# Output tile transposes one step later, down tiles gated by their own 512 tokens, one gate/up load moved ahead of the down stage

## Chip, cores and metric

The kernel runs as one program on the 8 NeuronCores of one Trainium2 chip. Each core computes 2048 of the 16384 tokens. There is no communication between the cores. The metric is the device time of the slowest core in microseconds (us). TensorE is called PE, VectorE DVE, ScalarE ACT, GpSimd POOL and SyncE SP.

## What is computed

The reference is one decoder layer; the stages before the output projection are untouched by the change and cut here to a line.

```python
# ... h = rms_norm(x); q, k, v, u, gates = h @ w_in; dilated attention; pooling;
# merged = gate_a * (o_attn @ w_proj_attn) + gate_p * (y_pool @ w_proj_pool)
x = x + rms_norm(merged @ w_out[l], g_post_mix[l])

h2 = rms_norm(x, g_pre_ffn[l])
gu = h2 @ w_gate_up[l]
a, b = gu[..., :FFN_HIDDEN], gu[..., FFN_HIDDEN:]
x = x + rms_norm((jax.nn.silu(a) * b) @ w_down[l], g_post_ffn[l])
```

D_MODEL is 1024 and FFN_HIDDEN is 2816. The products run in bf16 and accumulate in float32.

## The kernel before, in words

Every engine has its own list of instructions. The order on an engine is the order in which the Python code appends to its list, and an engine does them strictly in that order; a wait on a semaphore holds back everything that stands behind it on the same engine. The DMA issues of POOL and SP stand in these lists too.

**The output projection stage.** The 2048 tokens of a core are 16 tiles of 128. `wout_step(it)` is a software pipeline over them. In one step the parts work on different tiles:

- stage 1, tile `it`: SP loads the residual `xin` (four buffers), PE does the 16 matmuls of 128x512 with `wout` (L988) into one of three pairs of PSUM banks.
- add, tile `it-3`: POOL adds `tb` and `xin` into `x1b` (L1001, three buffers), SP stores `x1b` to `x1s` in DRAM.
- 2b1, tile `it-4`: ACT squares and sums `x1b` (L359) and the reciprocal root follows. For the first tiles it is a square root on ACT (L339) with a reciprocal on DVE (L340); for the last ones it is two small instructions on POOL (L341, L343).
- 2a, tile `it-1`: ACT squares and sums the matmul result in PSUM (L359), the same reciprocal root, and DVE scales the result into `tb` (L996).
- 2b2, tile `it-5`: DVE scales `x1b` to the bf16 tile `xs` (L1040, two buffers, named `xs2` in the code), PE transposes it in 8 instructions (L1048) into one of two PSUM banks, DVE copies it with a gain into `hT` (L1050).

A buffer of `x1b` may be written again when the `xs` made from it is done and its store has landed, so the add of tile n waits for the `xs` of tile n-3.

**The gate/up stage.** It follows twice (`hf` 0 and 1), each time for 1024 tokens, over 22 chunks j of 128 hidden columns and 2 blocks b of 512 tokens. A unit (j, b) is 8 matmuls for the gate (L1144) and 8 for the up part (L1147) in one of two pairs of banks. ACT does the SiLU into `sa` (L1158), DVE multiplies into `ffT` (L1159). The pair of banks is free again when this product is done. The weights of a chunk come by a DMA from the POOL list: `issue_gu(idx+2)` stands at the head of chunk `idx`, into one of three buffers, and waits until the last matmuls on that buffer are done. The same place issues one of the 22 pieces of `wdn`. The steps 16 to 20 of `wout_step` (no stage 1 any more) are mixed into the first five units: matmuls of the unit, then the step, then SiLU and product of the unit.

**The down stage.** After the 44 units of a half, 8 tiles of 128 tokens are multiplied with `wdn` (L1176, 44 matmuls of 128x512 each), followed by a norm on ACT, POOL and DVE, and by the residual add on POOL (L1001, into the same buffers `x1b`). Every down tile waits for this:

```python
ev_ff = dve.last()
...
pe.wait(frp, bank_free[pr_[0]], bank_free[pr_[1]], ev_wd, ev_ff)
```

`ev_wd` is the landing of all pieces of `wdn`; `dve.last()` is the product of the last unit (j = 21, b = 1).

Of the kernel before, what the change touches and what calls it, by code (L numbers as in the profile page):

```python
# [14 lines left out]
NT = T // 128  # L15
HT = 2048
FF = 2816
NJ = FF // 128
# [173 lines left out]
def build_program(taps=(), stop_after=None):  # L192
# [844 lines left out]
    def wout_stage2b2(st):  # L1037
        (i, b, ev_st, col2, ev_rs) = st
        b2 = i % 2
        ev_xs = dve.op(lambda e: e.tensor_scalar(out=xs2[b2][:, :], in0=x1b[b][:, :], scalar1=rsA[:, col2:col2 + 1], scalar2=None, op0=ALU.mult),  # L1040
                       waits=[ev_rs, xs2_free[b2]])
        x1b_free[b] = [ev_xs, ev_st]
        k_, bank, fr = tr_ring2.get()
        psb = ps[:, bank, :].bitcast(BF16).rearrange("p (k t) -> p k t", k=8)
        pe.wait(ev_xs, fr, bank_free[bank])
        ev_tr = None
        for k in range(8):
            ev_tr = pe.op(lambda e, k=k: e.transpose(out=psb[:, k, :], in_=xs2[b2][:, k * 128:(k + 1) * 128], identity=ident[:, :]), signal=(k == 7))  # L1048
        xs2_free[b2] = ev_tr
        ev_ev = dve.op(lambda e: e.tensor_tensor(out=hT[:, :, i * 128:(i + 1) * 128], in0=psb, in1=gffn[:, :].unsqueeze(2).to_broadcast([128, 8, 128]), op=ALU.mult),  # L1050
                       waits=[ev_tr])
        tr_ring2.release(k_, ev_ev)
        bank_free[bank] = ev_ev
        h2_ev[i] = ev_ev
# [3 lines left out]
    boot_ev = [pool.dma(wgu_boot[i][:, :, :, :], wgu_d[i], d_gub[i]) for i in range(2)]  # L1058
    d_wd = P.dsem("d_wd")
    ev_gf = sp.dma(gfin[:, :], gfin_d[:, :], P.dsem("d_gfin"))  # L1060
    st1, st2, st3, st4 = {}, {}, {}, {}

    def wout_step(it):
        if it < NT:
            st1[it] = wout_stage1(it)
        if 0 <= it - 3 < NT:
            st3[it - 3] = wout_stage2add(st2[it - 3])
        rstd_mode["act"] = it - 4 < 12
        if 0 <= it - 4 < NT:
            st4[it - 4] = wout_stage2b1(st3[it - 4])  # L1070
        rstd_mode["act"] = it - 1 < 15
        if 0 <= it - 1 < NT:
            st2[it - 1] = wout_stage2a(st1[it - 1])
        rstd_mode["act"] = False
        if 0 <= it - 5 < NT:
            wout_stage2b2(st4[it - 5])

    for it in range(NT):
        wout_step(it)
# [13 lines left out]
    fu = 0  # L1093
# [4 lines left out]
    def issue_gu(idx):  # L1098
        hf, j = loads[idx]
        b = idx % 3  # L1100
        ld_ev[idx] = pool.dma(wgu[b][:, :, :, :], wgu_d[j], d_gu[b], waits=[gu_free[b], ev_wout])
# [23 lines left out]

    def wgu_buf(idx):
        return wgu_boot[idx] if idx < 2 else wgu[idx % 3]
    for hf in range(2):
        for j in range(NJ):
            idx = hf * NJ + j  # L1130
            if 0 < idx < len(loads) - 2:
                issue_gu(idx + 2)
            if hf == 0 and j:
                ev_wd = pool.dma(wdn[:, j, :], wdn_d[:, j, :], d_wd)
# [2 lines left out]
            for b in range(2):  # L1137
# [10 lines left out]
                               signal=(k == 7))  # L1148
                if b == 1:
                    gu_free[wb] = e2  # L1150
                if hf == 0 and fu <= 5:
                    wout_step(NT + fu - 1)
                    if fu == 1:
                        issue_gu(2)
                        pool.dma(wdn[:, 0, :], wdn_d[:, 0, :], d_wd)
                    if fu == 5:
                        obuf_free = [x1b_free[0], x1b_free[1]]
                es = act.op(lambda e, ub=ub, ba=ba: e.activation(out=sa[ub][:, :], in_=ps[:, ba, :], func=AF.Silu), waits=[e1, sa_free[ub]])  # L1158
                ef = dve.op(lambda e, ub=ub, bb=bb, j=j, b=b: e.tensor_tensor(out=ffT[:, j, b * 512:(b + 1) * 512], in0=ps[:, bb, :], in1=sa[ub][:, :], op=ALU.mult),  # L1159
                            waits=[es, e2])  # L1160
                sa_free[ub] = ef
                ab_ring.release(ka, ef)
                bank_free[ba] = ef
                bank_free[bb] = ef
        ev_ff = dve.last()
        for il in range(8):
            i = hf * 8 + il
            b = i % 2
            ev_x1 = sp.dma(xin[b][:, :], x1s_d[i * 128:(i + 1) * 128, :], d_x1i[b], waits=[xin_free[b], x1_store_ev[i]])
            kp, pr_, frp = pair_ring2.get()  # L1170
            pe.wait(frp, bank_free[pr_[0]], bank_free[pr_[1]], ev_wd, ev_ff)
            ev = None
            evh = []
            for h2 in range(2):
# [110 lines left out]
```

How the kernel before makes its waits and increments, by code:

```python
    def wait(self, *evs):  # L40
        for ev in evs:
            if ev is None:
                continue
            if isinstance(ev, (list, tuple)):
                self.wait(*ev)
                continue
            key = id(ev.sem)
            if self.seen.get(key, 0) >= ev.val:
                continue
            self.seen[key] = ev.val
            sem, val = ev.sem, ev.val
            self.meta.append(("wait", id(sem), val))
            self.ops.append(lambda e, sem=sem, val=val: e.wait_ge(sem, val))
# [1 line left out]
    def op(self, fn, waits=(), signal=True):  # L55
        self.wait(*waits)
        if signal:
            self.count += 1
            sem, val = self.sem, self.count
            self.meta.append(("inc", id(sem), 1))
            self.ops.append(lambda e, fn=fn, sem=sem: fn(e).then_inc(sem, 1))
            return Ev(sem, val)
        self.ops.append(lambda e, fn=fn: fn(e))
        return None
# [4 lines left out]
    def dma(self, out, in_, dsem, waits=(), **kw):  # L69
        self.wait(*waits)
        dsem.count += 16
        sem = dsem.sem
        self.meta.append(("inc", id(sem), 16))
        self.ops.append(lambda e, out=out, in_=in_, sem=sem, kw=kw: e.dma_start(out=out, in_=in_, **kw).then_inc(sem, 16))
        return Ev(sem, dsem.count)
```

## Time and profile before

| what | value |
|---|---|
| time, median of 3 runs | 1025.14 us (1024.16 to 1026.15) |
| time of the profiled execution | 1024.68 us |
| span of its slowest core (core 2) | 1023.1 us |
| spans of the other cores | 1013.3 to 1021.0 us (core 5 is second) |
| PE busy on core 2 | 930.6 us (91% of the span) |
| output projection stage on core 2, first L988 to the last L1048 | about 475.8 to 565.7 us |
| first down stage, second gate/up stage, second down stage | from 701.3, 777.3 and 931.3 us |

The span is counted from the first to the last instruction of a core. The time of the execution is 1.6 us more than the span. Instruction times in the trace are start and duration in us from the span's start. The end of a PE instruction is modelled, so distances on PE are read here from start to start.

### The profile page before, as it was taken

The numbers are of one execution on the slowest core, as the hardware profiler recorded it, in microseconds if no ns is written. First come the engines' busy times: TensorE is split into PE (matmuls) and PEld (weight loads), VectorE is DVE, ScalarE is ACT, GpSimd is POOL, SyncE is SP. The second block draws the span as 40 slices with busy tenths as digits, with TensorE's granted clock in tenths as the row PEclk, the third lists the DMA queues.
The fourth block names the chain that finished last, engine by engine and source line by source line (L and its number), as shares of the span: only waits on it lengthen the run. The fifth ranks groups of instructions, "written<-read, shape, count | busy, mean of one in ns | idle before, by whom it ended". The sixth has DMA issues, their size and how long they took to land.

```text
span 1023.1 us, 15111 instructions; the slowest of 8 cores (1013.3 to 1023.1 us)
## 1 busy us (share of the span) xinstructions
PE 930.6 (91%) x5448; PEld 468.4 (46%) x5532; DVE 402.5 (39%) x554; ACT 342.2 (33%) x588; POOL 334.7 (33%) x324
## 2 busy tenths in 40 slices
PE   1569999999897999999898999999999999999993
PEld 0337554447674444444444444444444444444441
DVE  2465786548978433333576212121112112121111
ACT  3426663339777422223664111111101111111100
POOL 2462787663402343333456111111333000000331
PEclk9769999999998999999999999999999999999997
DMA  8879310000022171212977766762334544530322
GB/s 233 243 173 239 80 63 21 1 1 2 4 41 43 43 124 21 42 21 42 304 240 194 118 108 117 122 108 49 124 105 139 86 71 74 83 62 1 124 104 81
DMA packets 32586, 98.50 MB, mean 96 GB/s; under 512 B 4224, under 2 KB 4224, under 8 KB 32512
## 3 DMA queue, kind: packets, MB, share of 16 engines
q0 software_dynamic: 15296, 41.92, 24.8%
q1 hardware_dynamic: 17072, 55.58, 16.3%
q8 instruction: 45, 0.74, 0.3%
q14 instruction: 29, 0.24, 0.1%
q10 hardware_dynamic: 144, 0.03, 0.0%
HBM read 122.64 MB, written 16.78 MB: 136 GB/s over the span
## 4 chain that ended last, share of the span: by engine, by line
PE 80%; DVE 5%; DMA 4%; issue 4%; POOL 3%; ACT 3%; SPq 0%; DVEq 0%; ACTq 0%; POOLq 0%
PE ps L1176 14%; PE ps L1147 14%; PE ps L1144 14%; PE ps L438 12%; PE ps L925 6%; PE ps L928 5%; PE ps L518 5%; DMA xst<-xh 2%; PE ps L988 2%; PE ps L420 2%; PE ps L935 1%; PE ps L932 1%; PE ps L482 1%; DMA xin<-xo 1%; DVE tb L996 1%
## 5 line engine op out<-in xcount | busy, mean ns | idle before, releaser
L1144 PE MATMUL ps<-hT,wgu 128*128 128x512 bf16 x658 | 157.5, 379 | 1.5 <-DMA wgu<-wgu 0.7
L1147 PE MATMUL ps<-hT,wgu 128*128 128x512 bf16 x659 | 157.6, 379 | 0.7
L1176 PE MATMUL ps<-wdn,ffT 128*128 128x512 bf16 x690 | 151.5, 379 | 2.6 <-DVE ffT L1159 1.9
L1159 DVE TENSOR_TENSOR ffT<-ps,sa 128x512 bf16<-128x512 f32 x88 | 60.8, 691 | 226.2 <-PE ps L1147 226.2
L1158 ACT ACTIVATE sa<-ps 128x512 f32<-128x512 f32 x88 | 52.5, 597 | 247.3 <-PE ps L1144 247.3
L1176 PEld LDWEIGHTS ps<-wdn,ffT 128*128 128x128 bf16 x704 | 68.8, 98 | 85.4 <-issue 2.8
L1144 PEld LDWEIGHTS ps<-hT,wgu 128*128 128x128 bf16 x672 | 65.6, 98 | 79.8 <-issue 1.2
L1147 PEld LDWEIGHTS ps<-hT,wgu 128*128 128x128 bf16 x672 | 65.8, 98 | 79.3
L74 POOL DMA_DIRECT2D wgu<-wgu x42 | 22.5, 537 | 231.9 <-PE ps L1147 228.3
L1001 POOL TENSOR_TENSOR x1b<-tb,xin 128x1024 f32<-128x1024 f32 x31 | 72.8, 2348 | 58.3 <-DVE tb L996 29.9
L438 PE MATMUL ps<-hT,wqk 128*128 128x512 bf16 x374 | 89.4, 379 | 2.0 <-DVE uh L631 1.4
L498 POOL TENSOR_TENSOR kT<-t,t2b 128x512 bf16<-128x512 f32 (+1 forms) x36 | 65.4, 1826 | 47.3 <-DVE t2b L487 43.6
L359 ACT ACTIVATE junk<-ps 128x1024 bf16<-128x1024 f32 x31 | 31.7, 1022 | 142.4 <-PE ps L1176 132.4
L996 DVE SCALAR_TENSOR_TENSOR tb<-ps,rsA,gfin 128x1024 f32<-128x1024 f32 x15 | 19.3, 1284 | 131.2 <-POOL rsA L343 131.2
L947 POOL TENSOR_TENSOR mT<-m,m 128x512 bf16<-128x512 f32 x32 | 40.5, 1266 | 86.9 <-DVE m L942 86.9
L508 ACT ACTIVATE qb<-ps 128x512 bf16<-128x512 f32 (+1 forms) x60 | 35.0, 584 | 89.8 <-PE ps L438 88.2
L925 PE MATMUL ps<-hT,wgs 128*128 128x512 bf16 x249 | 60.5, 386 | 0.5 <-issue 0.2
L928 PE MATMUL ps<-hT,wgs 128*128 128x512 bf16 x250 | 60.4, 380 | 0.3
L420 PE MATMUL ps<-ident,xsb 128*128 128x128 bf16 x256 | 23.8, 249 | 40.2 <-ACT xsb L407 22.4
L941 DVE TENSOR_TENSOR m<-ps,sga 128x512 f32<-128x512 f32 x32 | 22.1, 692 | 93.6 <-PE ps L932 88.0
L438 PEld LDWEIGHTS ps<-hT,wqk 128*128 128x128 bf16 x384 | 37.1, 98 | 44.0 <-issue 1.3
L988 PE MATMUL ps<-wout,mT 128*128 128x512 bf16 x249 | 56.7, 379 | 0.4
(120 smaller groups left out, 1195.8 us busy)
## 6 DMA issues: line engine op xcount, KB each, us to landing
wgu<-wgu POOLq DMA_DIRECT2D x42, 512.0 KB, 5.1
xst<-xh SPq DMA_DIRECT2D x16, 512.0 KB, 18.0
xin<-xo SPq DMA_DIRECT2D x16, 512.0 KB, 5.4
x1s<-x1b SPq DMA_DIRECT2D x16, 512.0 KB, 3.9
xin<-x1s SPq DMA_DIRECT2D x16, 512.0 KB, 4.1
out<-x1b SPq DMA_DIRECT2D x15, 512.0 KB, 2.9
xst<-xo SPq DMA_DIRECT2D x12, 512.0 KB, 7.1
wdn<-wdn POOLq DMA_DIRECT2D x22, 256.0 KB, 6.1
```

The source lines that it names most:

```text
L438: ev = pe.op(lambda e, k=k: e.matmul(ps[:, bank, 0:n], lhsT=wfn(k), rhs=rhsfn(k), start=(k == 0), stop=(k == 7)), signal=(k == 7))
L498: ev_o = pool.op(lambda e: e.tensor_tensor(out=dst, in0=i0, in1=i1, op=ALU.add), waits=[ev_t1, ev_t2])
L518: ev = pe.op(lambda e, k=k: e.matmul(ps[:, bank, 0:256], lhsT=tok_ap_fn(k), rhs=wv_tile[:, g, k, :], start=(k == 0), stop=(k == 7)), signa ...
L925: e1 = pe.op(lambda e, k=k, wb=wb, b1=b1, tok=tok: e.matmul(ps[:, b1, :], lhsT=wgs[wb][:, 0, k, :], rhs=hT[:, k, tok], start=(k == 0), sto ...
L928: e2 = pe.op(lambda e, k=k, wb=wb, b2=b2, tok=tok: e.matmul(ps[:, b2, :], lhsT=wgs[wb][:, 1, k, :], rhs=hT[:, k, tok], start=(k == 0), sto ...
L988: ev = pe.op(lambda e, k=k, hf=hf, pr_=pr_: e.matmul(ps[:, pr_[0] + hf, :], lhsT=mT[:, k, i * 128:(i + 1) * 128], rhs=wout[:, k, hf * 512: ...
L1001: ev_o = pool.op(lambda e: e.tensor_tensor(out=outbuf[:, :], in0=tb[b][:, :], in1=xres[:, :], op=ALU.add), waits=[ev_t, ev_xres, out_free])
L1144: e1 = pe.op(lambda e, k=k, wbuf=wbuf, ba=ba, tok=tok: e.matmul(ps[:, ba, :], lhsT=wbuf[:, 0, k, :], rhs=hT[:, k, tok], start=(k == 0), st ...
L1147: e2 = pe.op(lambda e, k=k, wbuf=wbuf, bb=bb, tok=tok: e.matmul(ps[:, bb, :], lhsT=wbuf[:, 1, k, :], rhs=hT[:, k, tok], start=(k == 0), st ...
L1158: es = act.op(lambda e, ub=ub, ba=ba: e.activation(out=sa[ub][:, :], in_=ps[:, ba, :], func=AF.Silu), waits=[e1, sa_free[ub]])
L1159: ef = dve.op(lambda e, ub=ub, bb=bb, j=j, b=b: e.tensor_tensor(out=ffT[:, j, b * 512:(b + 1) * 512], in0=ps[:, bb, :], in1=sa[ub][:, :], ...
L1176: ev = pe.op(lambda e, j=j, h2=h2, pr_=pr_, il=il: e.matmul(ps[:, pr_[0] + h2, :], lhsT=ffT[:, j, il * 128:(il + 1) * 128], rhs=wdn[:, j, ...
```

## The change

Three things are changed, all in the last two thirds of a core's program. First, the 8 transposes of a tile and their copy into `hT` become a part of their own, `wout_stage2tr`, which handles tile `it-6` in step `it`, while the scaling to `xs` stays with tile `it-5`. The pipeline gets one more step, so the mixed part covers six units. Second, a down tile waits for the last product of its own 512 tokens. Third, the load with index 24 (chunk 2 of the second half) is issued ahead of the first down stage instead of at the head of the second gate/up stage.

```diff
@@ wout_stage2b2
         x1b_free[b] = [ev_xs, ev_st]
+        return (i, b2, ev_xs)
+
+    def wout_stage2tr(st):
+        (i, b2, ev_xs) = st
         k_, bank, fr = tr_ring2.get()
         psb = ps[:, bank, :].bitcast(BF16).rearrange("p (k t) -> p k t", k=8)
         pe.wait(ev_xs, fr, bank_free[bank])
@@ wout_step
         if 0 <= it - 5 < NT:
-            wout_stage2b2(st4[it - 5])
+            st5[it - 5] = wout_stage2b2(st4[it - 5])
+        if 0 <= it - 6 < NT:
+            wout_stage2tr(st5[it - 6])
@@ the gate/up and down stages
+    ev_ff = [None, None]
     for hf in range(2):
         for j in range(NJ):
             idx = hf * NJ + j
-            if 0 < idx < len(loads) - 2:
+            if 0 < idx < len(loads) - 2 and idx != NJ:
                 issue_gu(idx + 2)
...
-                if hf == 0 and fu <= 5:
+                if hf == 0 and fu <= 6:
                     wout_step(NT + fu - 1)
...
                 sa_free[ub] = ef
+                ev_ff[b] = ef
...
-        ev_ff = dve.last()
+        if hf == 0:
+            issue_gu(NJ + 2)
         for il in range(8):
...
-            pe.wait(frp, bank_free[pr_[0]], bank_free[pr_[1]], ev_wd, ev_ff)
+            pe.wait(frp, bank_free[pr_[0]], bank_free[pr_[1]], ev_wd, ev_ff[il // 4])
```

The first place is the PE list where the output projection ends and the gate/up units begin. L988 is stage 1, L1048 the 8 transposes of a tile, L1144 and L1147 the two halves of a unit; this is before:

```order
L988 MATMUL ps<-wout_119,mT_110 128x512 x96
L1048 MATMUL ps<-ident_43,xs_0_91_133 128x128 x8
L988 MATMUL ps<-wout_119,mT_110 128x512 x16
...
L988 MATMUL ps<-wout_119,mT_110 128x512 x16
L1048 MATMUL ps<-ident_43,xs_0_91_133 128x128 x8
L1144 MATMUL ps<-hT_54,wgub_95_137 128x512 x8
L1147 MATMUL ps<-hT_54,wgub_95_137 128x512 x8
L1048 MATMUL ps<-ident_43,xs_1_92_134 128x128 x8
L1144 MATMUL ps<-hT_54,wgub_95_137 128x512 x8
```

The same place in the changed kernel, where the transposes have L1052 and the unit L1151 and L1154:

```order
L988 MATMUL ps<-wout_119,mT_110 128x512 x112
L1052 MATMUL ps<-ident_43,xs_0_91_133 128x128 x8
L988 MATMUL ps<-wout_119,mT_110 128x512 x16
...
L988 MATMUL ps<-wout_119,mT_110 128x512 x16
L1052 MATMUL ps<-ident_43,xs_1_92_134 128x128 x8
L1151 MATMUL ps<-hT_54,wgub_95_137 128x512 x8
L1154 MATMUL ps<-hT_54,wgub_95_137 128x512 x8
L1052 MATMUL ps<-ident_43,xs_0_91_133 128x128 x8
L1151 MATMUL ps<-hT_54,wgub_95_137 128x512 x8
```

The first transposes stand behind seven tiles of stage 1 instead of six, and every later group stands one tile, or one unit, further back. The order on DVE within a step was scaling (L1040) of tile n, copy (L1050) of tile n; now it is scaling of tile n, copy (L1054) of tile n-1.

The second place is the POOL list around the first down stage. The last chunk of the first half issues a `wgu` and a `wdn` load; L341, L343 and L1001 are the norm and the add of a down tile. Before:

```order
L74 DMA wgu_100_142<-wgu 128x2048
L74 DMA wdn_121<-wdn 128x1024
L341 TENSOR_SCALAR msA_49<-ssA_48 128x1
L343 TENSOR_TENSOR rsA_50<-msA_49,nhalf_51 128x1
...
L1001 TENSOR_TENSOR x1b_86_128<-tb_89_131,xin_82_124 128x1024
L74 DMA wgu_98_140<-wgu 128x2048
L74 DMA wgu_99_141<-wgu 128x2048
```

In the changed kernel:

```order
L74 DMA wdn_121<-wdn 128x1024
L74 DMA wgu_98_140<-wgu 128x2048
L341 TENSOR_SCALAR msA_49<-ssA_48 128x1
L343 TENSOR_TENSOR rsA_50<-msA_49,nhalf_51 128x1
...
L1001 TENSOR_TENSOR x1b_86_128<-tb_89_131,xin_82_124 128x1024
L74 DMA wgu_99_141<-wgu 128x2048
```

The load of `wgu_98` (index 24) has moved ahead of the eight norms and adds; the list of SP is the same.

## Rows read from the trace of the kernel before

**Rows 1.** The page: the span; the chain that ended last, by engine

```profile
span 1023.1 us, 15111 instructions; the slowest of 8 cores (1013.3 to 1023.1 us)
...
PE 80%; DVE 5%; DMA 4%; issue 4%; POOL 3%; ACT 3%; SPq 0%; DVEq 0%; ACTq 0%; POOLq 0%
```

**Rows 2.** Waits of PE from 470 us on, core 2: total us, times, longest

```profile
PE ps L1048 <- DVE xs L1040: 8.0, 13, 2.5
PE ps L1176 <- DVE ffT L1159: 1.9, 2, 0.9
```

**Rows 3.** Timeline, one step: start, us, engine, line, what [idle before <-releaser]

```profile
502.90 0.61 PE L1048 MATMUL ps<-ident,xs 128*128 128x128 bf16 x8 [0.35 <-DVE xs L1040]
...
506.34 0.74 DVE L1040 TENSOR_SCALAR xs<-x1b,rsA 128x1024 bf16<-128x1024 f32 x1
...
507.23 0.61 PE L1048 MATMUL ps<-ident,xs 128*128 128x128 bf16 x8 [0.27 <-DVE xs L1040]
507.29 2.35 POOL L1001 TENSOR_TENSOR x1b<-tb,xin 128x1024 f32<-128x1024 f32 x1 [1.99 <-DVE xs L1040]
...
507.95 1.23 DVE L1050 TENSOR_TENSOR hT<-ps,cpk 128x1024 bf16<-128x1024 bf16 x1 [0.86 <-PE ps L1048]
```

**Rows 4.** Timeline, ACT and DVE from the add to the next scalings

```profile
494.46 0.20 ACT L339 ACTIVATE msA<-ssA 128x1 f32<-128x1 f32 x1
...
495.76 0.20 ACT L339 ACTIVATE msA<-ssA 128x1 f32<-128x1 f32 x1
...
497.60 0.74 DVE L1040 TENSOR_SCALAR xs<-x1b,rsA 128x1024 bf16<-128x1024 f32 x1
...
509.74 1.06 ACT L359 ACTIVATE junk<-x1b 128x1024 bf16<-128x1024 f32 x1 [0.99 <-POOL x1b L1001]
...
510.98 0.20 ACT L339 ACTIVATE msA<-ssA 128x1 f32<-128x1 f32 x1
```

**Rows 5.** Timeline, PE at the start of the stage

```profile
475.82 20.88 PE L988 MATMUL ps<-wout,mT 128*128 128x512 bf16 x94
...
498.49 0.61 PE L1048 MATMUL ps<-ident,xs 128*128 128x128 bf16 x8 [1.79 <-DVE xs L1040]
```

**Rows 6.** Timeline, PE: transposes of tile 14, and the seventh unit

```profile
561.21 0.61 PE L1048 MATMUL ps<-ident,xs 128*128 128x128 bf16 x8
...
569.01 1.89 PE L1144 MATMUL ps<-hT,wgu 128*128 128x512 bf16 x8
```

**Rows 7.** Timeline where the projection's last steps meet the first units

```profile
541.01 0.74 DVE L1040 TENSOR_SCALAR xs<-x1b,rsA 128x1024 bf16<-128x1024 f32 x1
...
546.37 1.28 DVE L996 SCALAR_TENSOR_TENSOR tb<-ps,rsA,gpost 128x1024 f32<-128x1024 f32 x1 [2.53 <-POOL rsA L343]
...
550.32 0.68 DVE L1159 TENSOR_TENSOR ffT<-ps,sa 128x512 bf16<-128x512 f32 x1
...
552.80 1.89 PE L1144 MATMUL ps<-hT,wgub 128*128 128x512 bf16 x8
...
554.24 2.37 POOL L1001 TENSOR_TENSOR x1b<-tb,xin 128x1024 f32<-128x1024 f32 x1
...
554.81 2.35 DVE L1040 TENSOR_SCALAR xs<-x1b,rsA 128x1024 bf16<-128x1024 f32 x1
```

**Rows 8.** Windows: PE, PEld, DVE, ACT, POOL busy (count), PEclk, DMA share, GB/s

```profile
498.00:541.50 43.50, 40.21 (x235) 19.44 (x240) 33.17 (x51) 27.37 (x62) 23.47 (x10) 1.00 0.77 270
```

**Rows 9.** Timeline and tile `wdn`: last piece issued and landed, first down tile

```profile
694.56 0.54 POOL L74 DMA_DIRECT2D wdn<-wdn  x1
...
698.51 1.89 PE L1147 MATMUL ps<-hT,wgu 128*128 128x512 bf16 x8
...
701.34 1.89 PE L1176 MATMUL ps<-wdn,ffT 128*128 128x512 bf16 x8 [0.95 <-DVE ffT L1159]
...
DMA to landing us min/median/max: 5.9/5.9/5.9
```

**Rows 10.** Timeline, PE: the first unit of chunk 2 in the second half

```profile
792.02 1.89 PE L1144 MATMUL ps<-hT,wgu 128*128 128x512 bf16 x8 [0.73 <-DMA wgu<-wgu]
```

More of the change, by code:

```diff
@@ L1060, in build_program @@
     ev_gf = sp.dma(gfin[:, :], gfin_d[:, :], P.dsem("d_gfin"))
-    st1, st2, st3, st4 = {}, {}, {}, {}
+    st1, st2, st3, st4, st5 = {}, {}, {}, {}, {}
     def wout_step(it):
```

## The prediction, as made before the changed kernel ran

> **What bounds the kernel now.** I read the page first, then the chain that ended last, then the waits of PE alone, then the timeline around each wait. The page says which core sets the time: core 2, span 1023.1, with PE on 80% of the chain [rows 1]. So a change pays only where PE stands still on core 2, or where something between its waits gets in PE's way. From 470 us on, the view of PE's waits has little in it [rows 2]: 13 waits of the transposes for the scaled tile, 8.0 us in all, and two waits of a down tile for the last product, 1.9 us. A third is a wait of 0.73 us for a weight load in the second gate/up stage [rows 10]. All three parts of the change are aimed at these, so the question for each is what is late next.
>
> Idle times on PE come from modelled ends, so I count from start to start. 96 matmuls take 20.88 us [rows 5], some 0.216 each once the last one's tail is taken off: 3.45 for the 16 of a tile or unit. Two units with their transposes take 7.80 (561.21 to 569.01, nothing waiting) [rows 6], so an undisturbed step is 3.90 and the 8 transposes are 0.45 of it. A step of the stage takes 4.33 now (502.90 to 507.23) [rows 3].
>
> **Why it is 4.33.** The timeline of a step shows a circle between PE and DVE: `xs` (506.34), then its transposes (507.23), then the copy to `hT` (507.95, DVE idle 0.86 for it), and behind the copy stand the reciprocals, `tb` and the next `xs` [rows 3]. DVE spends 4.33 - 0.86 = 3.47 of a step working or in short gaps. With the transposes one step back, the copy finds its transposes long done and PE finds its `xs` done: this circle falls to 3.47, under PE's 3.90.
>
> **What is late next in the stage.** The change leaves another circle, over two steps: the add waits for an old `xs`, and its result is squared on ACT ahead of the square from PSUM that the `tb` in front of a new `xs` needs. From `xs` of tile n to `xs` of tile n+2: 0.95 to the add (506.34 to 507.29), 2.45 to the square (509.74), 1.24 to its root (510.98) [rows 3, 4]; from this root to the root behind the PSUM square 1.30 (494.46 to 495.76), from there over reciprocal and `tb` to `xs` 1.84 (497.60) [rows 4]. Sum 7.78, or 3.89 a step. That is PE's pace by chance, so the stage should run at 3.90.
>
> **Part 1, the start.** `xs` of tile 0 starts at 497.60 [rows 4]. The six tiles of PE end their issue at 475.82 + 20.7 = 496.5; now PE waits until 498.49 [rows 5], afterwards it goes on with a seventh tile and reaches the first transposes at 500.0, when `xs` is done. Group n of the transposes then starts at 500.0 + 3.90 n, the one of tile 9 at 535.1, and the first unit at 535.5.
>
> **Part 1, the meeting with the units.** Here a new wait comes. The `xs` of tile 10 starts at 497.60 + 5 x 7.78 = 536.5; now it starts at 541.01 [rows 7]. From it to the `tb` of tile 15 the path is on POOL (the add, two small reciprocal-root pairs), because the last tiles don't use ACT's root: 546.37 - 541.01 = 5.36 [rows 7], which nothing in the change shortens. `xs` of tile 11 follows 1.20 later, at 543.1, is done at 543.8, then stand the copy of tile 10 (1.2, as in [rows 3]) and the product of unit 1 (0.68, [rows 7]), so unit 3, which needs unit 1's banks, starts at about 545.8. Undisturbed it would start at 535.5 + 2 x 3.90 = 543.3: a stall of 2.5 that stays. The row of unit 3 is now at 552.80 [rows 7]: gain 7.0. From unit 3 to unit 7 it is now 569.01 - 552.80 = 16.21 [rows 6, 7], afterwards 4 x 3.90 = 15.6 if each `xs` and product keeps ahead: another 0.6. The product of unit 2 should be done about 0.8 before unit 4 wants its banks, the product of unit 3 just in time for unit 5. Together 7.6.
>
> The added step costs no work: the same instructions, moved. The `xs` of tile n needs its buffer back from the transposes of tile n-2, which stand one step earlier, and the two transposing banks are freed by copies a full step back; neither has less than 2 us. PE's list is moved past no DMA of POOL or SP. The first units read `hT` of tiles 0 to 7, which are copied long before. The load for unit 5 stands on POOL behind the root of tile 15, so it is issued as much earlier as the `tb` is.
>
> **Part 2, the down tiles.** The last gate/up matmuls start at 698.51, so the first down matmul could start at 698.51 + 1.73 = 700.24; it starts at 701.34 [rows 9]: 1.10 to win. But the same wait holds the landing of the last `wdn` piece: issued at 694.56, landed 5.9 later at 700.46 [rows 9]. With the 0.15 from a releaser's end to PE's start (507.08 to 507.23) [rows 3], that is 700.6, so this part wins 0.74 here. Below it is 0 when the piece lands 0.8 later, above 1.10. On four other cores the wait is already the piece's; they are not the slowest. In the second half no piece is outstanding, and the two waits are alike (1.9 in two) [rows 2]: 1.10. The wait adds nothing in front of the other tiles.
>
> **Part 3, the load.** PE is idle 0.73 for it [rows 10], and by the down tile's example (0.95 idle, 1.10 from start to start) [rows 9] it is 0.15 more: 0.88. Issued ahead of the down stage, this load has over 75 us. POOL waits for the last unit's matmuls with it, which end before the first down tile is through, so no norm is held up. The next load waits for its own buffer as before. Nothing is late behind it.
>
> **Sum.** 7.6 + 0.74 + 1.10 + 0.88 = 10.3 on core 2. The profiled execution took 1024.68, so 1014.4; it lies 0.46 under the median of the runs shown, so the median should be 1014.8. The second slowest core, 2.1 us behind in span, has the same first two waits, so core 2 stays the slowest.
>
> **A rule against it.** A scaling that starts while POOL's add runs takes 2.35 instead of 0.74: it starts at 554.81, the add runs from 554.24 to 556.61, and the scaling ends 0.55 after it [rows 7]. The `tb` and the copies beside an add are not stretched. The Trainium skill says the same in "SBUF — State Buffer", section "Who interferes with whom": a DVE instruction in a mode with two ports and a GpSimd instruction exclude each other for their whole length, whoever comes first. By that rule the denser order would pay 1.6 us for each scaling that falls into an add; by the rows of the steady step it pays nothing, since the add begins after one scaling and ends before the next.
>
> **Rivals.**
> - *A: pace 4.1 and one or two stretched scalings among the units.* The two-step circle fits PE's pace with 0.02 to spare, so small delays stay. At 4.1 the `xs` of tile 10 starts 2.1 later; one or two stretched scalings (1.61 each) at units 4 and 5, less the slack of 0.8, add some 1.7. Then 1014.8 + 3.8 = 1018.6. Against it: each term was measured while other waits hid its best case.
> - *B: no stall at the units.* If the `tb` of tile 15 comes sooner, the 2.5 go too: 1012.3. Against it: POOL's part is in its list in order.
> - *C: the wait only moves and the step stays at 4.33.* Then parts 2 and 3 are all, 2.7 us: 1022.4. It needs a third circle that I don't see. DMA is busy 0.77 of the time [rows 8] and would have to reach 0.86 at the new pace; the loads of `xin` have some three steps.
> - *D, slower: every scaling falls into an add.* DVE's next scaling can start 3.47 after the last; the add is through 0.95 + 2.35 = 3.30 after it [rows 3]. If the adds start more than 0.17 later than that, the scaling waits for them, at most 1.61 each, and DVE's step is 5.08. Ten steps cost 11.9 against the forecast, one more at the units 1.6: 1028.3. It decides from 1.03 extra a step on. Against it: the adds wait for nothing but the `xs` in the steady steps, and PE's pace of 3.90 leaves 0.6.
>
> The clock does not enter: it is granted in full (1.00, the 2.4 GHz level) in this stretch [rows 8], and PE will idle less.
>
> **How the numbers follow.** The forecast has 0.70 (own range 1012.8 to 1016.8), A 0.13, B 0.07, C 0.05, D 0.05. From 1012.0 to 1018.6 lie B, the forecast and half of A and more, over 8 in 10. A measurement of this kernel can tell some 0.2%, 2 us, from nothing. Forecast, A and B are faster by more, C just about (0.27%), so faster 0.92, same 0.03, slower 0.05.
>
> **What would show it.** In the trace after: starts of transposes 3.90 apart from about 500 to 535 us; no DVE idle before the copy; POOL's add still released by `xs`; unit 3 started by the product of unit 1, some 2.5 late; the first down tile released by the `wdn` load and the ninth to start without a pause; no wait for a `wgu` load in the second half. I am wrong if the `xs` are over 4 us apart, if scalings of 2.35 show between 500 and 540, or if PE waits for `xs` again.

## The result, and the profile after

The changed kernel took 1013.74 us (median of 6 runs, 1011.59 to 1016.44), the kernel before 1024.41 beside it on the same chip (6 runs, 1023.67 to 1026.15). The ratio is 0.9896, with an interval of 0.9876 to 0.9917: 10.7 us faster, where the prediction's sum had 10.3. A second measurement on another occasion gave 0.9899 (0.9878 to 0.9921). The forecast of 1014.8 lies 0.1% above the median. Some executions of any of these kernels run in a slower state, at a lower granted clock on one die or both, and every time and ratio below is of the others.

The profiled execution took 1016.44, as long as any of the six. The page of the changed kernel, its span and the shares of its last chain:

```profile
span 1014.9 us, 15115 instructions; the slowest of 8 cores (1001.8 to 1014.9 us)
...
PE 81%; issue 4%; DVE 4%; DMA 3%; POOL 3%; ACT 2%; SPq 0%; DVEq 0%; POOLq 0%; ACTq 0%
```

The slowest core is now core 4, not core 2. Its waits of PE from 440 us on, changed kernel (total us, times, longest):

```profile
PE ps L1052 <- DVE xs L1040: 2.3, 2, 1.9
PE ps L1151 <- DVE ffT L1166: 1.2, 1, 1.2
PE ps L1185 <- DMA wdn<-wdn: 0.2, 1, 0.2
```

Against [rows 2] the 13 waits for the scaled tile have become 2, the down tiles' waits for a product are gone, and what is left is 0.2 for the last `wdn` piece and a new wait of a unit for a product, 1.2.

Timeline of core 4 in the changed kernel, two steps of the projection (start, us, engine, line, what, [idle before <-releaser]):

```profile
518.93 0.61 PE L1052 MATMUL ps<-ident,xs 128*128 128x128 bf16 x8
...
521.39 0.74 DVE L1040 TENSOR_SCALAR xs<-x1b,rsA 128x1024 bf16<-128x1024 f32 x1
...
522.05 1.22 DVE L1054 TENSOR_TENSOR hT<-ps,cpk 128x1024 bf16<-128x1024 bf16 x1
522.35 2.36 POOL L1001 TENSOR_TENSOR x1b<-tb,xin 128x1024 f32<-128x1024 f32 x1 [1.02 <-DVE xs L1040]
...
522.83 0.61 PE L1052 MATMUL ps<-ident,xs 128*128 128x128 bf16 x8
...
529.18 0.74 DVE L1040 TENSOR_SCALAR xs<-x1b,rsA 128x1024 bf16<-128x1024 f32 x1
```

The transposes are 522.83 - 518.93 = 3.90 apart and carry no wait (on this core one earlier step is 4.42, with a wait of 0.36); the copy to `hT` starts before them, right behind the scaling, where DVE idled 0.86 in [rows 3]. From a scaling to the one two tiles later it is 529.18 - 521.39 = 7.79, the two-step circle, still through the add that waits for `xs`.

Where the projection meets the units, changed kernel, core 4:

```profile
536.95 0.75 DVE L1040 TENSOR_SCALAR xs<-x1b,rsA 128x1024 bf16<-128x1024 f32 x1
...
542.32 1.28 DVE L996 SCALAR_TENSOR_TENSOR tb<-ps,rsA,gpost 128x1024 f32<-128x1024 f32 x1 [3.49 <-POOL rsA L343]
...
543.51 0.74 DVE L1040 TENSOR_SCALAR xs<-x1b,rsA 128x1024 bf16<-128x1024 f32 x1
...
544.41 0.61 PE L1052 MATMUL ps<-ident,xs 128*128 128x128 bf16 x8 [1.92 <-DVE xs L1040]
...
545.31 0.68 DVE L1166 TENSOR_TENSOR ffT<-ps,sa 128x512 bf16<-128x512 f32 x1
...
546.25 3.11 PE L1151 MATMUL ps<-hT,wgub 128*128 128x512 bf16 x8 [1.23 <-DVE ffT L1166]
...
549.02 3.17 DVE L1040 TENSOR_SCALAR xs<-x1b,rsA 128x1024 bf16<-128x1024 f32 x1
```

This is the forecast stall: the `tb` of tile 15 comes 542.32 - 536.95 = 5.37 after the scaling of tile 10 (5.36 in [rows 7]), idling for POOL's root, and unit 3 starts at 546.25, released by the product of unit 1. What was not forecast is in that row's own length: 3.11 for eight matmuls that take 1.89 elsewhere. The other half of the unit starts at 549.15 and the next transposes at 551.38, so the unit takes 5.13 from start to start instead of 3.45. Windows of the same core (us, then PE, PEld, DVE, ACT, POOL busy with counts, PEclk, DMA share, GB/s):

```profile
545.00:546.20 1.20, 0.01 (x1) 0.00 (x0) 1.20 (x3) 0.00 (x0) 1.20 (x1) 1.00 0.84 96
546.20:548.00 1.80, 1.75 (x6) 0.74 (x7) 1.80 (x2) 1.04 (x2) 1.56 (x3) 0.66 0.91 164
548.00:549.50 1.50, 1.50 (x5) 0.46 (x4) 1.50 (x3) 0.11 (x2) 1.49 (x4) 0.50 0.99 143
551.00:554.00 3.00, 3.00 (x21) 1.58 (x21) 3.00 (x4) 1.28 (x3) 2.45 (x5) 1.00 1.07 152
```

Behind the pauses of 1.92 and 1.23 the granted clock falls to 0.50, the 1.2 GHz level, and PE does 5 matmuls in 1.5 us; from 551 on it is 1.00 (2.4 GHz) again.

The other two parts, timeline of core 4: the first down tile of the first half, then that of the second half, then the first unit of chunk 2 in the second half.

```profile
693.03 1.89 PE L1154 MATMUL ps<-hT,wgu 128*128 128x512 bf16 x8
...
695.15 2.10 PE L1185 MATMUL ps<-wdn,ffT 128*128 128x512 bf16 x9 [0.23 <-DMA wdn<-wdn]
...
921.35 1.89 PE L1154 MATMUL ps<-hT,wgu 128*128 128x512 bf16 x8
...
923.07 3.18 PE L1185 MATMUL ps<-wdn,ffT 128*128 128x512 bf16 x14
...
783.21 1.89 PE L1154 MATMUL ps<-hT,wgu 128*128 128x512 bf16 x8
...
784.94 1.89 PE L1151 MATMUL ps<-hT,wgu 128*128 128x512 bf16 x8
```

The first waits for the last piece of `wdn`, as forecast; the other two follow the matmuls ahead of them after 1.72 and 1.73, without a pause.

**Where the time went, stretch by stretch.** Starts of PE, core 2 before against core 4 after, the slowest core of each profiled execution:

| stretch | before | after | difference | forecast |
|---|---|---|---|---|
| up to the stage (first projection matmul) | 475.82 | 474.74 | -1.08 | 0 |
| stage to unit 7 | 93.19 | 88.79 | -4.40 | -7.6 |
| unit 7 to the first down matmul | 132.33 | 131.62 | -0.71 | -0.74 |
| first down stage | 75.97 | 75.97 | 0 | 0 |
| second gate/up to second down | 153.95 | 151.95 | -2.00 | -1.98 |
| rest | 91.84 | 91.83 | -0.01 | 0 |

Sum -8.2, which is 1023.1 - 1014.9. The first line is not the change's: nothing in the diff stands ahead of it, and the stage starts anywhere from 465.55 to 474.74 on the eight cores of this one execution. Apart from it, what the forecast missed is in the second line.

**That line on all eight cores.** In the changed kernel four of them have the stage in 84.5 to 84.7, the others take 86.5 to 90.3. Two starts of DVE account for it: how late the first scaling comes (counted from the stage's first matmul), and how long scalings 0 to 10 take. The cleanest core has 20.57, 38.88 and 84.47; what a core has above the first two should come on top of 84.47.

| core | first scaling | scalings 0 to 10 | 84.47 and the two excesses | measured | left over |
|---|---|---|---|---|---|
| 0 | 21.26 | 41.51 | 87.79 | 89.36 | 1.57 |
| 1 | 20.58 | 38.87 | 84.47 | 84.47 | 0 |
| 2 | 20.57 | 38.88 | 84.47 | 84.47 | 0 |
| 3 | 21.73 | 40.79 | 87.54 | 90.29 | 2.75 |
| 4 | 22.77 | 39.44 | 87.23 | 88.79 | 1.56 |
| 5 | 20.58 | 38.90 | 84.50 | 84.52 | 0.02 |
| 6 | 20.85 | 38.87 | 84.74 | 84.72 | -0.02 |
| 7 | 22.19 | 39.35 | 86.56 | 86.54 | -0.02 |

Something is left over on cores 0, 3 and 4, and just these three show a granted clock under 1.00 between 530 and 554 us. The distance from unit 3 to unit 7 says the same without the table: 17.29, 18.48 and 17.28 on cores 0, 3 and 4, and 15.71 to 15.75 on the other five. So the half clock costs 1.6 to 2.8 where it comes. Before, it came on five cores in this stretch (0, 3, 4, 5, 6), but not on core 2, the only one whose clock stood in [rows 8]. In the second profiled execution of the changed kernel it came on two, 0 and 7.

Why the first scaling is late on core 4: the timeline of POOL and DVE at the start of the stage, changed kernel.

```profile
490.69 2.35 POOL L1001 TENSOR_TENSOR x1b<-tb,xin 128x1024 f32<-128x1024 f32 x1 [5.27 <-DMA xin<-xo]
...
497.51 0.74 DVE L1040 TENSOR_SCALAR xs<-x1b,rsA 128x1024 bf16<-128x1024 f32 x1
...
509.04 1.28 DVE L996 SCALAR_TENSOR_TENSOR tb<-ps,rsA,gpost 128x1024 f32<-128x1024 f32 x1 [0.52 <-POOL x1b L1001]
```

The second add waits 5.27 for its `xin`, and runs 15.95 after the stage's start; on cores 1, 2 and 5 it is 11.8 to 12.0. Later one `tb` waits 0.52 for an add to give back its buffer: most of the 0.56 by which this core's ten scalings are over 38.88. On core 0, where they are 2.63 over, rival D's collision is part of it. Timeline of core 0:

```profile
493.10 2.35 POOL L1001 TENSOR_TENSOR x1b<-tb,xin 128x1024 f32<-128x1024 f32 x1 [4.04 <-DMA xin<-xo]
493.53 2.47 DVE L1040 TENSOR_SCALAR xs<-x1b,rsA 128x1024 bf16<-128x1024 f32 x1
```

The third add is released by its `xin`, not by a scaling, and the first scaling falls into it and takes 2.47 instead of 0.74.

### The profile page after: what moved, and what is told of

Read it like the earlier page. It is cut to its first block, busy times and chain, and to the rows that moved or that the text cites. A ratio compares the mean times of both kernels' runs of the same rounds, so it can differ in the third digit from the quotient of the medians.

```text
span 1014.9 us, 15115 instructions; the slowest of 8 cores (1001.8 to 1014.9 us)
## 1 busy us (share of the span) xinstructions
PE 930.8 (92%) x5448; PEld 469.9 (46%) x5532; DVE 403.1 (40%) x554; ACT 341.2 (34%) x588; POOL 334.8 (33%) x324
## 4 chain that ended last, share of the span: by engine, by line
PE 81%; issue 4%; DVE 4%; DMA 3%; POOL 3%; ACT 2%; SPq 0%; DVEq 0%; POOLq 0%; ACTq 0%
PE ps L1185 15%; PE ps L1151 15%; PE ps L1154 15%; PE ps L438 12%; PE ps L925 6%; PE ps L928 5%; PE ps L518 5%; DMA xst<-xh 2%; DMA xin<-xo 2%; PE ps L420 2%; PE ps L935 1%; PE ps L932 1%; PE ps L482 1%; PE ps L792 1%; POOL x1b L1001 1%
## 5 line engine op out<-in xcount | busy, mean ns | idle before, releaser
L1151 PE MATMUL ps<-hT,wgu 128*128 128x512 bf16 x659 | 157.6, 379 | 0.7
L1154 PE MATMUL ps<-hT,wgu 128*128 128x512 bf16 x658 | 157.5, 379 | 0.7
L1185 PEld LDWEIGHTS ps<-wdn,ffT 128*128 128x128 bf16 x704 | 68.8, 98 | 83.5 <-issue 0.7
L1154 PEld LDWEIGHTS ps<-hT,wgu 128*128 128x128 bf16 x672 | 65.8, 98 | 79.3
L1151 PEld LDWEIGHTS ps<-hT,wgu 128*128 128x128 bf16 x672 | 65.6, 98 | 78.6
L1001 POOL TENSOR_TENSOR x1b<-tb,xin 128x1024 f32<-128x1024 f32 x31 | 72.9, 2350 | 55.0 <-DVE tb L996 27.9
L988 PE MATMUL ps<-wout,mT 128*128 128x512 bf16 x249 | 56.4, 379 | 0.4
```

The costliest lines, as they stand in the source:

```text
L988: ev = pe.op(lambda e, k=k, hf=hf, pr_=pr_: e.matmul(ps[:, pr_[0] + hf, :], lhsT=mT[:, k, i * 128:(i + 1) * 128], rhs=wout[:, k, hf * 512: ...
L1001: ev_o = pool.op(lambda e: e.tensor_tensor(out=outbuf[:, :], in0=tb[b][:, :], in1=xres[:, :], op=ALU.add), waits=[ev_t, ev_xres, out_free])
L1151: e1 = pe.op(lambda e, k=k, wbuf=wbuf, ba=ba, tok=tok: e.matmul(ps[:, ba, :], lhsT=wbuf[:, 0, k, :], rhs=hT[:, k, tok], start=(k == 0), st ...
L1154: e2 = pe.op(lambda e, k=k, wbuf=wbuf, bb=bb, tok=tok: e.matmul(ps[:, bb, :], lhsT=wbuf[:, 1, k, :], rhs=hT[:, k, tok], start=(k == 0), st ...
L1185: ev = pe.op(lambda e, j=j, h2=h2, pr_=pr_, il=il: e.matmul(ps[:, pr_[0] + h2, :], lhsT=ffT[:, j, il * 128:(il + 1) * 128], rhs=wdn[:, j, ...
```

## The experiments

Each kernel ran beside the kernel before: the first four beside a median of 1025.59, the next four beside 1024.53, the last four beside 1026.02. "The stage" below is from the first projection matmul to unit 7: before 91.9 to 94.9 on the eight cores, after 84.5 to 90.3.

### Part 1 alone, and parts 2 and 3 alone

From the changed kernel, the waits and the load put back:

```diff
-            if 0 < idx < len(loads) - 2 and idx != NJ:
+            if 0 < idx < len(loads) - 2:
-        if hf == 0:
-            issue_gu(NJ + 2)
-            pe.wait(frp, bank_free[pr_[0]], bank_free[pr_[1]], ev_wd, ev_ff[il // 4])
+            pe.wait(frp, bank_free[pr_[0]], bank_free[pr_[1]], ev_wd, ev_ff[1])
```

> Transposes one step later alone; down tiles and load as before. My theory (three waits that add up): the stage from the first projection matmul to the seventh gate/up unit has 84.5 us on cores without a late start and 88 to 90 on the others, as in the changed kernel, against some 92 to 95 before; the first down tile again waits 1.1 us from start to start for the last product, the second too, and the load of chunk 2 of the second half costs up to 0.9. In all 8 us faster than before, about 1016. Rival (the gain comes mainly from the down stage and the load, the stage only shifts its wait): under 4 us faster than before.

And only these hunks, in their new form, on the kernel before:

> The down tiles' own wait and the early load alone; transposes as before. My theory: the stage keeps its length of before (92 to 95 us to the seventh unit); from the seventh unit to the first down tile it is 0 to 0.7 shorter, the stretch from the second gate/up stage to the second down stage is 1.1 to 2.0 shorter at 151.95 us on every core. Together 2 to 2.7 us faster, about 1022. Rival as above: 6 us or more faster.

Part 1 alone: 1016.7 (1014.39 to 1019.17), ratio 0.9916 (0.9892 to 0.9939), so 8.6 us. The stage takes 84.4 to 89.8, as in the changed kernel. Parts 2 and 3 alone: 1023.57, ratio 0.9984 (0.9964 to 1.0003), so 1.6 us with an interval that just holds none; in its trace the second gate/up stage takes 151.95 on all eight cores (153.1 to 154.4 before). From unit 7 to the first down tile it is 131.95 to 133.69 against 132.33 to 133.59 before, so the gain of part 2 at the first down tile doesn't show over the cores. The stage, in which this kernel is the one before, takes 93.5 to 97.6, with a clock that falls on seven cores: that alone hides most of the gain in a single execution. The two add to 10.2 against 10.7 for the whole. No interplay of the parts shows, though the intervals, 2 us either way, would hide one of 1 us.

In part 1 alone the late load shows what it can cost. Core 2, timeline of PE and a window around it:

```profile
781.15 3.26 PE L1151 MATMUL ps<-hT,wgu 128*128 128x512 bf16 x8 [2.11 <-DMA wgu<-wgu]
784.20 2.25 PE L1154 MATMUL ps<-hT,wgu 128*128 128x512 bf16 x8
```

```profile
776.00:790.00 14.00, 11.89 (x49) 4.92 (x47) 1.76 (x3) 1.79 (x3) 0.53 (x1) 0.88 0.75 136
```

A wait of 2.11, and behind it eight matmuls in 3.26 and a mean clock of 0.88: this core's stretch takes 157.01. On the three cores of this kernel without a wait for the load it is 153.05 or 153.06, with part 2's 1.10 still in it. The late load thus costs 3.96 here: 2.26 for the wait from start to start, and 1.7 for the clock (the unit behind it takes 5.13 from start to start instead of 3.45). Part 3 takes away not only the 0.9 that core 2 paid before, but a cost that reaches 4 us when a pause and the clock come together.

### The roots of the last tiles on ACT

The 5.36 on POOL stays because the last tiles take their roots there. One more tile of each kind takes it on ACT:

```diff
-        rstd_mode["act"] = it - 4 < 12
+        rstd_mode["act"] = it - 4 < 13
-        rstd_mode["act"] = it - 1 < 15
+        rstd_mode["act"] = it - 1 < 16
```

> The changed kernel, with the reciprocal roots of the last projection tile and of the x1b of tile 12 on ACT and DVE instead of POOL. My theory (the stall that is left at the units is POOL's add and two root pairs ahead of tb of tile 15): the scaling of tile 11 comes 2.2 us sooner, PE waits 0 for it and about 1.2 for the product of unit 1 before unit 3 instead of 1.9 and 1.2 on the slow-starting cores; where the clock is granted at half after this stall now (1.7 us or more lost on cores 0, 3, 4) it stays full. Slowest core 2 to 4 us shorter than the changed kernel, some 1010 to 1011. Rival (the stall hangs on the two-step circle over the add and the squares): the scaling of tile 11 moves by less than 0.5 us and the time is that of the changed kernel.

1011.67 (1011.14 to 1011.94), ratio 0.9868 (0.985 to 0.9886): by the ratios 2.8 us less than the changed kernel, with intervals that still touch. Core 6, timeline at the meeting with the units:

```profile
533.75 0.74 DVE L1040 TENSOR_SCALAR xs<-x1b,rsA 128x1024 bf16<-128x1024 f32 x1
...
536.93 1.28 DVE L996 SCALAR_TENSOR_TENSOR tb<-ps,rsA,gpost 128x1024 f32<-128x1024 f32 x1 [0.17 <-DVE rsA L340]
...
538.13 0.74 DVE L1040 TENSOR_SCALAR xs<-x1b,rsA 128x1024 bf16<-128x1024 f32 x1
539.67 0.61 PE L1052 MATMUL ps<-ident,xs 128*128 128x128 bf16 x8
...
540.86 1.89 PE L1151 MATMUL ps<-hT,wgub 128*128 128x512 bf16 x8 [0.58 <-DVE ffT L1166]
```

The `tb` comes 3.18 after the scaling instead of 5.37, the next scaling 4.38 instead of 6.56; the transposes have no wait and unit 3 has 0.58 left. The stage takes 83.1 on four cores and 84.0 on three; no core's clock falls in it. Core 0 has 86.5: its first scaling takes 2.23 beside an add, and its scalings 0 to 10 take 41.25. So POOL's root chain sets the length of the stall at the units, and with the stall the half clock goes. The chain from one scaling to the next has a second link, the add that waits for a scaling, and the experiment with a fourth buffer below cuts that one.

The same edit on the kernel before:

> The kernel before with the same roots on ACT and DVE, nothing else. My theory: the steps stay 4.33 us apart, the wait of 2.5 us ahead of the second unit shrinks to under 0.5, later waits stay; 2 to 2.5 us faster than before, about 1022. It says what of the gain of the change could have been had without moving the transposes. Rival (the step length of 4.33 comes from POOL's work): the step length changes too.

1020.93, ratio 0.9963 (0.9948 to 0.9978): 3.8 us, more than expected. The stage takes 89.7 to 92.8 against 91.9 to 94.9 before, so 2.2 of it are seen there, and the clock falls on no core at the units. Core 5, timeline:

```profile
533.86 0.75 DVE L1040 TENSOR_SCALAR xs<-x1b,rsA 128x1024 bf16<-128x1024 f32 x1
534.75 0.61 PE L1048 MATMUL ps<-ident,xs 128*128 128x128 bf16 x8 [0.27 <-DVE xs L1040]
...
538.19 0.75 DVE L1040 TENSOR_SCALAR xs<-x1b,rsA 128x1024 bf16<-128x1024 f32 x1
539.08 0.61 PE L1048 MATMUL ps<-ident,xs 128*128 128x128 bf16 x8 [0.27 <-DVE xs L1040]
```

The steps stay 4.33 apart with 0.27 of idle each: this circle does not depend on the roots. In the changed kernel, which moves the transposes, it is gone.

### A fourth buffer for the sum

The two-step circle runs through the add, whose buffer the scaling gives back. A fourth buffer cuts it:

```diff
-        xb = i % 3
+        xb = i % 4
```

(with the buffer `x1b3`, its semaphore and its place in the list of free events)

> The changed kernel with a fourth buffer x1b, so that an add waits for the scaling four tiles back. My theory (on cores with a late start the scalings run in a circle over two tiles, 7.78 us for two, anchored at the first scaling, and never catch up): the circle now spans three tiles, so after a late first scaling the later ones come closer to PE (scaling of tile 10 about 1.5 us sooner after the first one than the 39.4 now), and the small waits of 0.2 to 0.4 in the steps go; the stage is 1 to 2 us shorter on the late cores, no change on the others. Rival D of the prediction (adds that are free to start fall on the scalings): scalings of up to 2.35 us show in the steps and the steps pass 4.0 us.

1012.4 (1011.36 to 1012.86), ratio 0.9874 (0.9852 to 0.9897). Scalings 0 to 10 take 37.5 to 38.3 instead of 38.9 and the next follows 4.18 later. The roots are still on POOL, and yet that next scaling comes 2.4 sooner than in the changed kernel (6.56): the stall needs both the add's wait and the root chain. The stage takes 83.3 to 84.8, without a fallen clock, and also the clean cores gain (83.3 for 84.5), which was not expected. At the start of the stage the adds are released by `xin`, and rival D's collisions appear. Core 0, timeline:

```profile
491.61 4.81 POOL L1001 TENSOR_TENSOR x1b<-tb,xin 128x1024 f32<-128x1024 f32 x2 [1.79 <-DMA xin<-xo]
...
494.29 2.67 DVE L1040 TENSOR_SCALAR xs<-x1b,rsA 128x1024 bf16<-128x1024 f32 x1
...
497.11 0.61 PE L1052 MATMUL ps<-ident,xs 128*128 128x128 bf16 x8 [1.27 <-DVE rsA L340]
...
497.97 2.35 POOL L1001 TENSOR_TENSOR x1b<-tb,xin 128x1024 f32<-128x1024 f32 x1 [1.55 <-DMA xin<-xo]
...
498.47 2.40 DVE L1040 TENSOR_SCALAR xs<-x1b,rsA 128x1024 bf16<-128x1024 f32 x1
```

Scalings of 2.67 and 2.40, each ending 0.5 behind an add. That agrees with the Trainium skill, "SBUF — State Buffer", section "Who interferes with whom": of a two-port DVE instruction and a GpSimd one, the later is shut out until the first is through. The first of them is done at 496.96 and its transposes start at 497.11, 25.61 after the stage's start instead of 24.18: PE waits 1.27 for it (the row names the reciprocal right behind the scaling as releaser), so here a collision costs PE 1.4 us. Cores 3, 4 and 6 have one wait of 0.9 to 1.1 each beside such scalings, the other four none. The kernel is no slower for it: by the ratios it is 2.2 us under the changed kernel, within the intervals. In the steady steps of both kernels every add waits for a scaling, and that keeps the two apart.

### Transposes two steps behind

```diff
-        b2 = i % 2
+        b2 = i % 3
-        if 0 <= it - 6 < NT:
-            wout_stage2tr(st5[it - 6])
+        if 0 <= it - 7 < NT:
+            wout_stage2tr(st5[it - 7])
-                if hf == 0 and fu <= 6:
+                if hf == 0 and fu <= 7:
```

(with a third `xs2` buffer)

> The changed kernel with the transposes two steps behind the scaling and a third xs buffer. My theory (behind the transposes stands the product of unit 1, which is late by itself because tb of tile 15 is): PE no longer waits for a scaling, but waits as much longer for the product of unit 1 before unit 3; the time is that of the changed kernel within 0.2%. Rival (the transposes' own wait is what is left): another 2 us off on the late cores.

1015.49, ratio 0.9907 (0.9883 to 0.9932): no better than one step, as expected. PE never waits for `xs`, but core 5, timeline:

```profile
538.40 0.68 DVE L1166 TENSOR_TENSOR ffT<-ps,sa 128x512 bf16<-128x512 f32 x1
...
539.34 2.31 PE L1151 MATMUL ps<-hT,wgub 128*128 128x512 bf16 x8 [3.29 <-DVE ffT L1166]
```

The whole stall now stands ahead of unit 3, 3.29 in one piece: slack between scaling and transposes doesn't help a product that is queued behind the late `tb` on DVE.

### The boot loads behind the second add

To test the late first scaling: the two 512 KB loads `wgu_boot` go out behind the second add instead of ahead of the stage.

```diff
-    boot_ev = [pool.dma(wgu_boot[i][:, :, :, :], wgu_d[i], d_gub[i]) for i in range(2)]
+    boot_ev = []
+            if it - 3 == 1:
+                boot_ev.extend(pool.dma(wgu_boot[i][:, :, :, :], wgu_d[i], d_gub[i]) for i in range(2))
```

> The changed kernel with the two loads of the first gate/up chunks (1 MB) issued on POOL behind the second add instead of ahead of the stage. My theory (cores differ by how late the xin tile of the second add lands while these loads share the DMA engines): the second add starts 2 to 4 us sooner on the late cores, the first scaling no more than 20.6 us after the first projection matmul, and all cores have the stage of 84.5 to 86 us; slowest core 2 to 4 us shorter. Rival (the second add waits for memory that all cores share, whatever this core loads): the second add is no sooner, the time the same.

The second add now starts 14.3 to 14.4 after the stage's start and the first scaling 20.57, on all eight cores (11.8 to 15.9 and 20.57 to 22.77 in the changed kernel). The stage takes 84.4 to 85.8 and the clock stays. So these loads are what spread the start. Three cores then have 40.1 to 40.3 for scalings 0 to 10, the other excess of the table above: 84.47 + 1.3 is about the 85.7 to 85.8 that they measure. On one of them, core 1, an add waits 3.34 for a store of `x1b` to land, and a scaling beside that add takes 1.15. The kernel as a whole shows no gain: 1014.82 (three executions), ratio 0.9898 (0.9858 to 0.9938). The slowest core of its profiled execution has an ordinary stage, but started it at 476.07. The 2 to 4 us that I expected are not shown; the interval, 4 us either way, doesn't exclude 2.

### The best of these together

A further small edit issues the `wdn` piece of a chunk ahead of the `wgu` load that waits for a buffer on the same queue (in the changed kernel the first down tile starts 131.6 to 132.1 after unit 7, in its second profiled execution up to 133.4):

```diff
-            if 0 < idx < len(loads) - 2 and idx != NJ:
-                issue_gu(idx + 2)
             if hf == 0 and j:
                 ev_wd = pool.dma(wdn[:, j, :], wdn_d[:, j, :], d_wd)
+            if 0 < idx < len(loads) - 2 and idx != NJ:
+                issue_gu(idx + 2)
```

First with the ACT roots and the late boot loads:

> The changed kernel with the roots of the last tiles on ACT, the late boot loads, and each piece of wdn issued ahead of the gate/up load of its chunk instead of behind it. My theory: the three add up; the first down tile starts without a pause (0.2 to 0.7 us), unit 3 waits at most 1.2, no core has the clock at half in the stage. About 5 us under the changed kernel on the slowest core, 1008 to 1010. Rival (the slowest core is set by what happens ahead of the stage, so that savings here move the median little): under 2 us.

The ratio is 0.9857 (0.9819 to 0.9895), from two executions, 1009.76 and 1011.21. The stage takes 83.1 to 83.5 on all cores, and unit 7 to the down stage 131.23 on six of them. Core 6 has 132.45: there PE waits 1.07 for a `wgu` load, which may be the price of issuing `wdn` first. In the three kernels below no core waits so.

Then, beside the changed kernel run once more: ACT roots, `wdn` first and the fourth buffer; ACT roots, `wdn` first and late boot loads (the kernel of the last experiment again); and all four edits.

> The changed kernel once more, as the measure for the three beside it on the same chip. All theories: ratio to before 0.988 to 0.992; scaling of tile 10 comes 38.87 us after the first one on most cores, 6.56 from the scaling of tile 10 to that of tile 11 on all.

> The changed kernel with the roots of the last tiles on ACT, each wdn piece ahead of its gate/up load, and four x1b buffers. My theory (the stall at the units is the root chain on POOL; late cores are held by the circle through the add): no half clock in the stage, 83.1 to 84.5 us from the first projection matmul to the seventh unit on all cores, no pause at the first down tile. 3 to 5 us under the changed kernel. Rival (adds that are free to start fall on the scalings and eat the gain): over 84.5 us on the late cores and no better than roots alone (3 us under the changed kernel).

> The changed kernel with the roots on ACT, the wdn pieces first and the two boot loads behind the second add (the combination of before, measured in more rounds). My theory: stage 83.1 to 83.5 us on all cores, 131.23 us from the seventh unit to the first down tile where no gate/up load is late; 3 to 5 us under the changed kernel. Rival (the wdn pieces in front delay the gate/up loads of the first half): waits for wgu loads of about 1 us on several cores eat half of the 0.2 to 0.7 won at the first down tile.

> All four: roots on ACT, wdn first, late boot loads, four x1b buffers. My theory: as the kernel with late boot loads, since cores without a late first scaling gain nothing from the fourth buffer (83.1 to 83.5 us for the stage); within 0.2% of it. Rival (the fourth buffer pays by itself): 1 us or more under it.

| kernel | median us | ratio to before |
|---|---|---|
| changed kernel again | 1015.49 | 0.9899 (0.9878 to 0.9921) |
| roots, wdn, fourth buffer | 1009.11 | 0.9847 (0.9823 to 0.9871) |
| roots, wdn, boot loads | 1009.58 | 0.984 (0.9815 to 0.9866) |
| all four | 1009.13 | 0.984 (0.9815 to 0.9865) |

With all four edits, the page and a window of core 2 over the stage:

```profile
span 1007.7 us, 15208 instructions; the slowest of 8 cores (1000.7 to 1007.7 us)
```

```profile
470.00:530.00 60.00, 60.00 (x339) 29.66 (x338) 41.92 (x65) 38.51 (x88) 36.13 (x19) 1.00 0.87 281
530.00:556.00 26.00, 26.00 (x158) 13.25 (x157) 17.93 (x21) 8.68 (x14) 11.39 (x16) 1.00 0.95 170
```

PE is busy without a gap, the view of its waits is empty on all eight cores from 440 us on, and the stage takes 83.12 on every one. That is what its matmuls need: 22 groups of 3.45 and 16 of transposes of 0.45 make 83.1. A scaling of 2.92 still occurs in this kernel, at no cost to PE. The three combinations can't be told apart, and each takes 0.5 to 0.6% less than the changed kernel. In all three unit 7 to the first down matmul is 131.23 on every core. What is left between cores lies ahead of the stage: it starts at 466.4 to 473.3.

## Why the prediction was right, and where it was not

**Right, by its own steps.** Core 4 and the clean cores (1, 2, 5 and 6, with the stage in 84.5 to 84.7) show them:
- The circle between PE and DVE is gone, the transposes stand 3.90 apart (but for one step on core 4), and the two-step circle gives 38.87 for ten scalings on four cores, where 5 x 7.78 = 38.9 was forecast. The first transposes start 24.17 or 24.18 after the stage does on every core, the forecast's 500.0 - 475.82. Rivals C (steps of 4.33) and A's pace of 4.1 are out on the clean cores.
- The stall at the units is there with its cause, 5.37 against 5.36, and the edit of the roots takes most or all of it away, so rival B, no stall, is a kernel of its own and not a way in which this one goes.
- Rival D's collisions don't occur in the steady steps of the profiled core. They occur at the start of the stage on core 0 (a first scaling of 2.47) and, with the fourth buffer, cost PE up to 1.4 us on a core, but they don't decide the time of either kernel. One scaling among the units is stretched to 3.17, as rival A has it, but PE doesn't wait for it.
- Parts 2 and 3: 0.71 measured for 0.74, 2.00 for 1.98.

**Wrong: the size of the stage's term, 7.6 against 4.40 in the profiled execution.** The forecast median was nearly met all the same, since that execution is 2.7 us above the median of its six; part 1 alone was worth 8.6 by its ratio, with an interval of 6.3 to 11.1. That the total came within 0.1% is partly luck: the slowest core lost 3.2 against the forecast, the clean cores won 1.1 over it, and the sum knew of neither. The 3.2 on core 4 come from three places:
1. *"`xs` of tile 0 starts at 497.60"*, 21.78 after the stage's start. It is 22.77 here: 0.99. The forecast took one core's start for a constant; over the cores it is 20.57 to 22.77, and it sets the path to the stall one to one.
2. *"5 x 7.78"* was 39.44 here, 0.54 more, of which 0.52 is one `tb` that waits for an add. Small delays of this kind stay, as rival A's text said.
3. *"The clock does not enter ... and PE will idle less."* This is the step that failed; the first two are sizes. PE idles less in sum, but in the forecast's own stall it idles 1.92 and 1.23 close together, and the clock then falls to the 1.2 GHz level. By the table this costs 1.56; unit 3 to unit 7 takes 17.28 here where 15.6 was forecast. I had read the clock on core 2 alone and only up to 541.50, ahead of the meeting with the units; on five other cores it had fallen there before.

0.99 + 0.54 + 1.6 is the 3.2, within 0.1. On the clean cores the stage takes 84.5, a little less than the 93.19 - 7.6 = 85.6 of the forecast, because their first scaling is 1.2 earlier.

**One of its signs was set wrong.** "If PE waits for `xs` again" was to show the prediction wrong, and PE does wait for it here, 1.92 on core 4 at the units. But the forecast's own path has such a wait: with `xs` of tile 11 done at 543.8 and unit 3 due at 543.3, the transposes in front of that unit are late.

**"Core 2 stays the slowest" was wrong too.** From unit 7 on the cores take nearly equal times, so the slowest is the one with the latest start and the longest stage together. In this execution that is core 4 (474.74 and 88.79), while core 2 started at 465.55 and ended first.

**Still open.** Why the clock falls on some cores only: it fell on cores 0, 3 and 4, with pauses at the units of 1.92, 2.40 and 1.92 and another of 1.23 behind each, but not on core 7 with 1.75 and 1.24. With the transposes two steps behind it fell behind single pauses of 4.70 and 3.29 and not behind 3.34, 3.17 or 3.08, so the length of the pause alone doesn't tell. Whether the boot loads delay `xin` by sharing queues or memory: moving them evens out the start, and more was not tried. And what makes the start of the stage differ by 7 to 10 us from core to core, which now decides which one ends last.

## What to carry to other kernels

When a wait is taken away, work out the next circle from start to start and then ask what sets its first turn: here the circle was right to a hundredth, and the first scaling and the stall behind the last one, on POOL, were what varied. Read such a stage on all cores, not only on the slowest: which core is slowest can change, and the others show how wide each term is. Price a short pause of PE by more than its length where other cores show a fallen clock behind a like one; here, where the clock fell, it cost from half to four fifths of the pauses on top of them (1.6 behind 1.92 and 1.23, 1.7 behind 2.11). An edit with no gain in the time that can be told from noise (parts 2 and 3) can still be read in its own stretch of the trace: 151.95 on all eight cores for 153.1 to 154.4.

## What the runs showed of the hardware that was not expected

- TensorE's clock fell from the 2.4 to the 1.2 GHz level behind pauses of 1.9 and 1.2 us in an otherwise full stretch: on 3 of 8 cores in the changed kernel, at 1.6 to 2.8 us each, and on 2 of 8 in its second profiled execution; on 5 of 8 before. With parts 2 and 3 alone, where the old stall stands, on 7. It fell on none in the stage with the roots on ACT. Behind a single pause of 2.11 it cost 1.7 us more (two halves of a unit in 5.13 instead of 3.45).
- Two 512 KB loads issued ahead of the stage spread the start of the second add over 11.8 to 15.9 us from core to core. Issued behind it, all eight cores had 14.3 to 14.4.
- POOL's own small work suffers beside a scaling too: on core 4 a root's first instruction takes 0.51 at 546.90, beside the scaling of 545.91, and 0.18 at 540.34 without one.
